# Attention stage of a streaming encoder step: order of copies and sums, masks of the streams by another route, and copies moved in two SSM groups

## The reference, cut to what matters

```python
h = rmsnorm(x, norm_mix[0])
q, k, v, qi, ki, wi = split(h @ w_in)            # attention inputs and indexer inputs
s = einsum('bqhd,bsd->bqhs', qi, keys_i)         # 8 indexer heads
score = einsum('bqhs,bqh->bqs', relu(s), wi) * IDX_SCALE
score = where(k_chunk <= q_chunk, score, -inf)
top_s, top_i = lax.top_k(score, min(256, n_keys // 4))
logits = q . k[top_i] * ATTN_SCALE + bias_tab[rel_bucket(top_i - pos)]
out = softmax(logits) @ v[top_i]                 # 16 heads on 4 key/value heads
x = x + out @ w_o
x = x + square(relu(rmsnorm(x) @ w_up)) @ w_down
h = rmsnorm(x)
xs, B, C, z, dt = conv_silu_split(h @ ssm_w_in)  # 8 groups
y, state = ssd_scan(xs, dt, A, B, C, state0)
x = x + gated_norm(y, z) @ ssm_w_out             # then the second MLP and the last norm
```

## Time and profile before

| | before |
|---|---|
| median of 3 timed runs | 1880.13 us (1877.41 to 1880.49) |
| profiled execution, its own time | 1876.36 us |
| its span | 1874.6 us |
| busy share: PE, DVE, ACT, POOL | 98%, 67%, 43%, 15% |
| mean granted TensorE clock | 0.995 of full |

### The profile page before, as it was taken

The page is one execution under the profiler, slowest core; times in us unless marked ns, Lnnn a source line. Parts: engine busy times, 40 slices in busy tenths (PEclk is TensorE's granted clock), DMA queues, the critical chain, the costliest instruction groups (busy, mean ns, idle before and its releaser), DMA issues.

```text
span 1874.6 us, 35518 instructions
## 1 busy us (share of the span) xinstructions
PE 1834.3 (98%) x13290; PEld 1731.4 (92%) x13290; DVE 1259.0 (67%) x2359; ACT 802.1 (43%) x1436; POOL 290.1 (15%) x336
## 2 busy tenths in 40 slices
PE   8999889999999999999999999999999999999998
PEld 7877556999999999999999999998999999999998
DVE  4488875348668585447788788888444766858653
ACT  4232674334343343335455644556333434434332
POOL 0001541110000000122323434233011000000001
PEclk9999999999999999999999999999999999999999
DMA  6363215232323223222443344434423231322321
GB/s 156 83 109 67 64 36 151 53 90 74 96 63 98 78 68 96 85 57 87 133 120 115 118 131 145 129 116 161 135 78 90 68 102 57 96 74 80 93 66 57
DMA packets 311427, 176.88 MB, mean 94 GB/s; under 512 B 39744, under 2 KB 304896, under 8 KB 310272
## 3 DMA queue, kind: packets, MB, share of 16 engines
q1 hardware_dynamic: 308464, 171.95, 32.5%
q10 hardware_dynamic: 2832, 3.15, 0.5%
HBM read 155.17 MB, written 19.72 MB: 93 GB/s over the span
## 4 chain that ended last, share of the span: by engine, by line
PE 88%; DVE 4%; issue 3%; ACT 3%; DMA 0%; DVEq 0%; POOL 0%; SPq 0%; ACTq 0%
PE psum L208 32%; PE psum L1380 27%; PE psum L1426 14%; PE psum L592 1%; PE psum L2474 1%; PE psum L2567 1%; PE psum L2487 1%; PE psum L556 1%; PE psum L596 1%; PE psum L2501 1%; PE psum L543 1%; PE psum L2405 1%; PE psum L568 1%; PE psum L2591 1%; DVE conv_out L711 0%
## 5 line engine op out<-in xcount | busy, mean ns | idle before, releaser
L208 PE MATMUL psum<-b2H,WH 128*128 128x320 f32 x912 | 218.0, 320 | 0.3 <-DVE b2L L1186 0.3
L208 PE MATMUL psum<-b2H,WL 128*128 128x320 f32 x912 | 209.0, 311 | 0.0
L208 PE MATMUL psum<-b2L,WH 128*128 128x320 f32 x912 | 208.8, 310 | 0.0
L196 ACT ACTIVATE WH<-W 128x1024 fp32r<-128x1024 f32 x90 | 95.1, 1056 | 214.9 <-PE psum L208 207.1
L1380 PE MATMUL psum<-b2H,HT 128*128 128x320 f32 x816 | 186.2, 309 | 0.0
L1380 PE MATMUL psum<-b2L,HT 128*128 128x320 f32 x816 | 186.0, 309 | 0.0
L1426 PE MATMUL psum<-HH,HT 128*128 128x320 f32 x544 | 167.4, 308 | 1.5 <-DVE HL L1515 1.5
L1426 PE MATMUL psum<-HL,HT 128*128 128x320 f32 x544 | 167.8, 308 | 0.0
L208 PEld LDWEIGHTS psum<-b2H,WH 128*128 128x128 f32 x912 | 150.1, 190 | 8.0 <-issue 7.3
L208 PEld LDWEIGHTS psum<-b2H,WL 128*128 128x128 f32 x912 | 153.5, 189 | 0.0
L208 PEld LDWEIGHTS psum<-b2L,WH 128*128 128x128 f32 x912 | 153.4, 189 | 0.0
(11 more groups left out here) (407 smaller groups left out, 4335.4 us busy)
## 6 DMA issues: line engine op xcount, KB each, us to landing
W<-ssm_w_in SPq DMA_DIRECT2D x98, 256.0 KB, 3.1
RW<-mlp_w_up SPq DMA_DIRECT2D x64, 256.0 KB, 3.1
RWx<-mlp_w_up SPq DMA_DIRECT2D x64, 256.0 KB, 3.1
RW<-mlp_w_down SPq DMA_DIRECT2D x64, 256.0 KB, 3.1
RWx<-mlp_w_down SPq DMA_DIRECT2D x64, 256.0 KB, 3.2
bc<-scratch_acs SPq DMA_DIRECT2D x8, 1280.0 KB, 7.7
W<-attn_w_in SPq DMA_DIRECT2D x32, 256.0 KB, 4.0
prev<-state_ssm SPq DMA_DIRECT2D x16, 512.0 KB, 5.6
```

What stands on the lines that cost most here:

```text
L196: act.activation(WH[:, b.slot], W[:, b.slot], ACT.Copy).then_inc(w_hi, 1)
L208: last = pe.matmul(psum[0:m, b.out + h, 0:TH], w[:, b.slot, k, 0:m], r[:, k, h * TH:(h + 1) * TH], start=(n == 0 and i == 0), stop=(n == K ...
```

## The change

**Start.** On ACT x_hi(7) now stands ahead of x_squares(3); on DVE the last chunk_lo stands ahead of the norm's reciprocal. A constant of 512 KB (c_rep) is no longer loaded, nor cast by POOL.

**Q blocks.** The index sums of two samples are made together: Rs has room for two, sum_heads works once per pair of samples and writes rows 0 to 31 and 32 to 63 of one PSUM bank (sel is 32 columns wide, 16 of them zero), copy_scores copies 64 rows once per pair. The top-k's first round reads the scores where they are, without the copy into WK, and its last round leaves out the replacement.

**Prompt attention.** The transposes of two units of a pair with t at most 1 go to one PSUM bank, and one copy takes both. spread_sums moves between the two logits of its step, copy_spread one unit later. scale_heads writes to hF, and heads_hi and heads_lo move into the sample attention, one tile per sample. The samples' top-k has 33 steps in place of 34 and starts without its copy; their mask steps come one unit earlier and write float32 into WKs.

**Sample attention.** The mask product on PE is gone. Instead SP stores the whole mask to memory (264 KB), and for every sample loads the rows with each repeated for its heads (264 KB); POOL adds them to the bias (BMs), two additions of 128x528 per sample, and sample_max takes BMs in place of biasS. The loop over samples is written out.

**SSM.** In the first group Btok is copied ahead of silu_rows(3), in the last one copy_prev(7, 0) ahead of exp_w.

```diff
-            sp.dma_start(rep_stage[:], A["c_rep"].rearrange("p (b r) -> p b r", b=DB)).then_inc(rep_in, 16)
...
+            def load_mask(b):
+                sp.wait_ge(bm, NU + max(2 * b - 2, 0))
+                sp.dma_start(MS[:, b % 2],
+                             skew(S["scores"], DS * b * KEYS_S, [[0, 8], [KEYS_S, DS], [1, KEYS_S]])
+                             ).then_inc((ss_in, bias_in)[b % 2], 16)
+
             sp.wait_ge(mk, 28)
+            sp.dma_start(S["scores"], WKs[:]).then_inc(tb_out, 16)
+            sp.wait_ge(tb_out, 32)
+            load_mask(0)
+            load_mask(1)
             sp.wait_ge(qz, 1)
             for s in range(2):
                 load_v(s, s)
-            with sp.Fori(1, DB // 2) as i:
...
+            for b in range(2, DB):
+                sp.wait_ge(skt, 2 * b - 2)
+                load_k(b, b % 2)
+                load_mask(b)
+                sp.wait_ge(pv, NPV + 2 * b - 2)
+                load_v(b, b % 2)
...
+            def sample_bias(b):
+                pool.wait_ge((ss_in, bias_in)[b % 2], (16, 256)[b % 2] + 16 * (b // 2) + 16)
+                for a in range(2):
+                    if b:
+                        pool.wait_ge(ttr, NU + 2 * b + a - 1)
...
+                    pool.tensor_tensor(BMs[:, a], MS[:, b % 2], biasS[:, a], ALU.add).then_inc(bm, 1)
...
-            def sum_heads(b, bank_=7):
-                pe.wait_ge(iR, b + 2)
-                pe.matmul(psum[0:DS, bank_, 0:512], sel[:], Rs[:, 0:512], start=True, stop=True)
-                pe.matmul(psum[0:DS, 6, 32:32 + DS], sel[:], Rs[:, 512:KEYS_S], start=True, stop=True).then_inc(isl, 1)
+            def sum_heads(i, bank_=7):
+                pe.wait_ge(iR, 2 * i + 3)
+                for s in range(2):
+                    pe.matmul(psum[32 * s:32 * s + 32, bank_, 0:512], sel[:], Rs[:, s, 0:512], start=True, stop=True)
+                for s in range(2):
+                    last = pe.matmul(psum[32 * s:32 * s + 32, 6, 32:32 + DS], sel[:], Rs[:, s, 512:KEYS_S], start=True, stop=True)
+                last.then_inc(isl, 1)
...
                 for q in range(t + 1):
-                    last = pe.transpose(psum[:, 4 + u % 2, q * P:(q + 1) * P], PR[:, u % 4, q * P:(q + 1) * P], ident)
+                    c = (2 * q + gp if in_pair(u) else q) * P
+                    last = pe.transpose(psum[:, turned_bank(u), c:c + P], PR[:, u % 4, q * P:(q + 1) * P], ident)
...
                 if u + 4 < NU:
                     logits(u + 4)
-                    logits(u + 5)
                 if u % 8 == 0 and u:
                     spread_sums(u // 8 - 1)
+                if u + 4 < NU:
+                    logits(u + 5)
...
                 for lo, n in ((0, 512), (512, DS)):
                     out = psum[:, 2 * a + lo // 512, 0:n]
-                    pe.matmul(out, repst[:], maskS[:, lo:lo + n], start=True, stop=False)
-                    last = pe.matmul(out, qst[:, a], kpT[:, a, lo:lo + n], start=False, stop=True)
+                    last = pe.matmul(out, qst[:, a], kpT[:, a, lo:lo + n], start=True, stop=True)
...
             for t in range(NT):
-                if t < 3:
+                if t < 4:
                     x_hi(t + 4)
                 x_squares(t)
...
             norm_act_sqrt(act, 0)
-            x_hi(7)
...
-                if u % 8 == 1 and u > 8:
+                if u % 8 == 2 and u > 8:
                     copy_spread(u // 8 - 1)
-                if u % 8 == 4 and u > 8:
-                    heads_hi(u // 8 - 1)
...
+            for b in range(DB):
+                if b:
+                    sample_heads(b - 1)
                 sample_turned(b)
+                heads_hi(b)
...
+            chunk_lo(dve, 7, 7, 0, b1H, b1L)
             norm_dve_recip(dve, 0)
-            chunk_lo(dve, 7, 7, 0, b1H, b1L)
...
             def sample_max(b, a):
                 dve.wait_ge(qk, NU + 2 * b + a + 1)
+                dve.wait_ge(bm, NU + 2 * b + a + 1)
...
-                dve.tensor_tensor_reduce(PRS[:, a], bank(2 * a, KEYS_S, 2), biasS[:, a], -1.0, -LOWEST,
+                dve.tensor_tensor_reduce(PRS[:, a], bank(2 * a, KEYS_S, 2), BMs[:, a], -1.0, -LOWEST,
...
-        silu_rows(act, g, 3)
+        if not g_is_first(g):
+            silu_rows(act, g, 3)
         act.wait_ge(tB, g + 1)
...
         act.activation(Btok[:], bank(4, T, 2), ACT.Copy).then_inc(bt_, 1)
+        if g_is_first(g):
+            silu_rows(act, g, 3)
...
         exponents(act, g, between)
+        if last:
+            copy_prev(act, SG - 1, 0)
         exp_w(act, g)
```

More of the change, by code:

```diff
@@ L72, in shape_constants @@
     c[:, 640:648] = i[:, None] // DS == np.arange(DB)[None, :]
-    rep = np.zeros((P, DB, P), np.float32)
-    for b in range(DB):
-        for r in range(P):
-            rep[DS * b + r % DS, b, r] = 1.0
-    sel = np.zeros((P, DS), np.float32)
+    sel = np.zeros((P, 32), np.float32)
     sel[i, i % DS] = 1.0
@@ L418, in build, with in_pair, turned_bank, turned_free @@
     NPV = NU // 2
+    def in_pair(u):
+        return UNITS[u][1] <= 1
+    def turned_bank(u):
+        return 4 + (u // 2 % 2 if in_pair(u) else u % 2)
+    def turned_free(u):
+        last = max(p for p in range(u // 2 * 2) if turned_bank(p) == turned_bank(u))
+        return last // 2 * 2 + 2 if in_pair(last) else last + 1
     LAST_PAIR = 3
@@ L2219, in _ @@
                     load_slab(sp, Block(n), slab_o(P * (n - B_O)))
-                if b:
+                if b and b % 2 == 0:
+                    store_scores(b - 2)
                     store_scores(b - 1)
@@ L2440, in mid @@
                     turn_ki(i, s, first and s == 0)
-                    if not (first and s == 0):
-                        sum_heads(2 * i + s - 1)
+                    if not first and s == 0:
+                        sum_heads(i - 1)
                 for s in range(2):
                     multiply(pe, Block(B_Q + s, i), b1H, b1L, between=lambda: mid(s))
-                    index_sample(2 * i + s)
+                    index_sample(i, s)
             q_pair(0, True)
@@ L2522, in _ @@
             turn_kv(0, 4)
-            pe.wait_ge(isc, 2 * DB)
+            pe.wait_ge(isc, DB)
             turn_kv(1, 7)
-            sum_heads(DB - 1, 5)
+            sum_heads(3, 5)
             for u in range(0, NU, 2):
@@ L2712, in copy_ki, with copy_scores @@
                 act.activation(kiP[:, 0:PAST], bank(4), ACT.Copy).then_inc(ik, 1)
[L2714 to L2718 removed]
+            def copy_scores(i, bank_=7):
+                act.wait_ge(isl, i + 2)
+                for s in range(2):
+                    act.wait_ge(iss[s], 16 * i + 16)
+                act.activation(selo[:, 0:512], psum[0:64, bank_, 0:512], ACT.Copy).then_inc(isc, 1)
+                act.activation(selo[:, 512:KEYS_S], psum[0:64, 6, 32:32 + DS], ACT.Copy).then_inc(isc, 1)
             def q_pair(i, first=False):
@@ L2722, in q_pair @@
                     copy_ki(2 * i + s)
-                    if s:
-                        copy_scores(i, 0)
-                    elif not first:
-                        copy_scores(i - 1, 1)
+                    if s == 0 and not first:
+                        copy_scores(i - 1)
                     b = Block(B_Q + 2 + s, i)
@@ L2753, in copy_turned @@
                 _, t, j, gp = UNITS[u]
+                if in_pair(u) and gp == 0:
+                    return
                 act.wait_ge(tp, u + 1)
-                if u == 0:
-                    act.wait_ge(iss[0], 16 * (DB // 2 + 1))
-                if u == 8:
+                if u == 9:
                     act.wait_ge(ss_in, 16)
                 wait(act, pv, u // 2 - 1)
+                if in_pair(u):
+                    act.activation(PT[:, u // 2 % 2, 0:t + 1].rearrange("p t g q -> p (t g q)"),
+                                   bank(turned_bank(u), 2 * P * (t + 1)), ACT.Copy).then_inc(pte, 2)
+                    return
                 act.activation(PT[:, u // 2 % 2, 0:t + 1, gp],
@@ L2764, in copy_spread @@
                 act.wait_ge(rsp, w + 1)
-                wait(act, otl, w)
+                wait(act, oe, w)
                 act.activation(OT[:], bank(7), ACT.Copy).then_inc(rbc, 1)
@@ L2813, in _ @@
             copy_spread(NU // 8 - 1)
-            heads_hi(NU // 8 - 1)
             sample_exp(0, 0)
@@ L2946, in q_block @@
                 split_lo(dve, Block(B_Q + 2 + s, i))
-                weigh_index(2 * i + s)
-            top_round(0)
+                weigh_index(i, s)
+            top_round(0, first=True)
             top_round(1)
@@ L2957, in _ @@
             top_round(14)
-            top_round(15)
+            top_round(15, last=True)
             q_block(3, 1)
@@ L3110, in _ @@
             scale_heads(NU // 8 - 1)
-            heads_lo(NU // 8 - 1)
             sample_max(0, 0)
@@ L3125, in sample_step @@
                 sample_normalize(b)
+                heads_lo(b)
                 if not last:
@@ L3129, in _ @@
             dve.wait_ge(qz, 4)
-            sample_step(0)
```

(3 more changed lines are left out.)

169 lines of the change are left out of this document (75 added, 94 removed).

## The result

| | before | changed |
|---|---|---|
| median of the timed runs | 1879.79 us (1877.41 to 1880.49, 4 runs) | 1860.91 us (1859.92 to 1862.98, 4 runs) |
| ratio | | 0.9911 (0.9896 to 0.9926) |
| span of the profiled execution | 1874.6 us | 1858.1 us |

The change saves 18.9 us where 31.6 were forecast. The time is inside the range by 0.1 us, but by the ratio (0.9911 of 1880.13 is 1863.4) it is outside. It is a gain, and six tenths of the forecast one by the medians; by the ratio it is 16.7 us, and the two traces differ by 16.5. One execution of a later run, start_undone, took 8286.73 us and is left out of its ratio.

The account below looks back on a forecast made before the run. PE, busy 98% of the span, was taken as the bound. Terms 5.2 + 5.3 + 8.0 + 5.5 + 3.7 + 3.8 = 31.5 us off 1876.4, plus 3.8 for the median, gave 1848.5 us; range 1842 to 1861.

Parts of the forecast that it names:

- Start: First stage: x_hi(7) earlier removes PE's 1.8 us wait for b1L and 3.4 us of lower clock, 5.2 us.
- Q blocks: Index sums made in pairs save 4.0 us, the vanished wait for Rs 1.3: 5.3 us (1.3 to 5.3).
- the rival of tiles in a row: Q blocks: a pair's products in two column tiles run one after another, 4.0 us stay, 1852.5 us; chance 0.07.
- the forecast's own bound: Q blocks: if paired sums run in a row, 7 single become 3 double ones and 1.0 us of saving remains.
- Prompt attention: PE's 16 waits for exponentials at seven tile boundaries go: 8.0 us (5 to 9.5).
- with spreading half a step earlier on PE: Prompt attention: this and the copy one unit later give ACT another exponential meanwhile, part of the 8.0 us.
- Sample attention: Mask products gone from PE save 4.3 us, the stage's start 1.2: 5.5 us (2 to 6).
- the 1.2 at the start: Sample attention's start: 1.2 us saved because heads_lo no longer stands there.
- the 0 to -1 that was named: Sample attention's start: possible loss of 0 to 1 us by the chain of mask store, load and POOL's addition.
- SSM: Waits for Btok (first group) and prevT (last group) shrink, with the clock behind them: 3.7 and 3.8 us.
- the waits go over to DVE or to POOL's chain: Prompt attention gives only 3 of 8.0 us, sample attention 2 of 5.5: 1857 us; chance 0.22.
- The clock still drops: Lower clock stays at the start and both SSM places, up to 6.8 us lost: 1850 to 1855 us; chance 0.15.

Follow-up runs that it names:

- start_undone: Changed kernel with the first stage's old order (x_hi(7) behind the square root, last chunk_lo behind the reciprocal): 1864.65 us, ratio 0.9935.
- before_rows: Kernel before the change, with the SSM's skip weights read as 128 packets of 64 bytes, not 2,048 of 4; also called the control: 1876.7 us, ratio 1.0001.
- copy_back: best_guess with copy_spread one unit earlier on ACT, where it was before the change: 1857.28 us, ratio 0.9896.
- d_in_rows: Changed kernel with the SSM's skip weights read as 128 packets of 64 bytes, not 2,048 of 4 (skip values wrong): 1854.26 us, ratio 0.9877.
- fill: Changed kernel with 18 transposes into an unused bank in PE's waits at the end of the sample attention: 1853.25 us, ratio 0.9875.
- d_split: Changed kernel with the second half of the skip weights' 4-byte load issued behind the last W_o slab: 1851.62 us, ratio 0.9864.
- best_guess: Changed kernel with spread_sums behind both logits, skip weights' load in two halves apart, second mask's load behind the values: 1849.34 us, ratio 0.9858.
- spread_first: Changed kernel with spread_sums ahead of both logits of its step: 1860.02 us, ratio 0.9909.
- spread_behind: Changed kernel with spread_sums back behind both logits of its step: 1859.65 us, ratio 0.9903.

## Why the prediction was right in its parts and wrong in its sum

- **Start (5.2, measured 5.9).** Right: the wait and the lower clock behind it are gone, and come back with the order. The size holds within a microsecond only, since the same wait was followed by 3.4 us at the lower clock in before_rows and by 6.8 in the kernel before.
- **Q blocks (5.3, measured 6.1).** Right. A pair of sums in two column tiles takes 1.05 us, x4 (the row above), where a single one took 1.03, x2; the rival of tiles in a row is out. Its price was wrong by the forecast's own bound, which leaves 1.0 of the 4.0: 3.0 would have stayed, not 4.0.
- **Prompt attention (8.0, measured 4.2).** Half of the mechanism was right, and by copy_back its size too: the copy one unit later is worth 8.5. The step that failed is "with spreading half a step earlier on PE": I took it as a help at no price. PE's two logits of a pair use rows 0 to 63 and 64 to 127 and run side by side; set between them, spread_sums makes each run alone. Undone, the stretch is 3.6 us shorter, and 7.8 shorter than before the change, where 8.0 were forecast. In the Q blocks I had asked whether two narrow products run side by side, and here I did not ask what the move would part, though the x4 rows of the trace show it.
- **Sample attention (5.5, measured 3.7).** A size: a round is 6.49 us where it was 7.03, so 0.54 less, as forecast (twice 0.27), but in six rounds only; they gave 3.2, against 4.3 forecast for the mask products of eight; and of the 1.2 at the start 0.5 is left, since 0.85 went into DVE's wait for POOL, within the 0 to -1 that was named. The load took 4.6 us rather than the 2.8 of the earlier trace rows, the store 2.1 rather than 2.8. All eight heads_lo took 0.69 us, and none fell beside an addition of POOL, so whether the two exclude each other was not put to the test here.
- **W_o (0, measured -8.8).** The step that failed, and the one that cost the most, is the sum's silence: a stage that isn't changed was taken as fixed, at nothing, without a reason. 5.5 us of wait and 1.7 of clock behind it come from the fetch of PE's instructions, held back for some 17 us by 4-byte packets (d_in_rows, fill, d_split and the control show it). The earlier trace rows show what stands behind such packets, 19.7 us for a load of 16 KB, and the prediction used that row for the masks only. The other 1.6, the clock at the start of W_o, is lower in some executions: 0.67 in the changed kernel's profile, 1.00 in best_guess, with the same waits of PE ahead (0.54, 0.36, 0.75 and 0.99 us), and before_rows has it as well, without any of the change. The two are not quite a sum: spread_first and start_undone have the full clock there, but a wait of 5.9, and take 36.3 and 36.0 us where the changed kernel takes 37.0. So the fetch alone costs 7.7 to 8.1, and the clock at the start adds 0.7 to 1.0 more.
- **SSM (7.5, measured 7.1).** Right: prevT's wait became 0.47, for the states, 0.4 having been forecast.
- **The rest (0, measured -1.7).** The MLPs run 1.2 and 0.5 us longer over 500 us each. The offset of 3.8 between the profiled execution and the median was 1.0 for the changed kernel. And the forecast's 1844.9 + 3.8 is 1848.7, not 1848.5. No experiment here tells the first two from chance.

With the two failed steps at what was measured, 31.5 - 3.6 - 7.2 = 20.7 and less the 1.8 in the sample attention 18.9, which is the gain by the medians; that it fits to the digit is luck, as the clock's 1.6 and the surplus of the first stages cancel, and by the ratio the gain is 16.7. Of the rivals, "the waits go over to DVE or to POOL's chain" had 0.22 and a time of 1857; its amount in the prompt attention was about right and its cause wrong: neither DVE nor POOL is what held PE. "The clock still drops" did not come true in its three places, but in two others. No rival named what cost the most.

## What to carry to other kernels

When an instruction is moved on PE, look at what stands on both sides of the gap: two products on different rows or columns of the array cost the time of one here, and with other products between the two of a pair on different rows they cost the time of two. Before transfers in packets of 4 bytes are laid beside straight-line code, ask which engine's next instructions fall due in that time; keep a run of such packets short (here two of 10 us did no harm where one of 20 cost 7 us) or read the data in rows. A wait labelled "issue" in the middle of unbroken work, with weights and inputs there, is worth a look at the instruction queues of the DMA view.

## What the runs showed of the hardware

- 2,048 packets of 4 bytes ran at about 106 per us from 309 to 329 us and kept the 16 DMA engines busy for 4.7% of their time. Still, what came behind, two loads of 16 KB and the packet of queue 8, landed only when they were nearly done (20.7 us for the first, against 2.9 without them). One packet of instructions of another queue, 14, did get through at 315.0 us.
- PE ran on for about 14 us (an estimate, above) after the fetch that was held back had fallen due.
- The granted clock behind like waits of PE is not the same from one execution to the next. After waits of 0.39, 0.88 and 0.96 us at the prompt attention's head, d_in_rows and spread_behind had 0.58 from 175 to 180 us, the changed kernel, fill and best_guess 1.00; that is some 2.6 us, as much as some of the terms that one would like to tell apart. At the start of W_o, behind the waits named above, seven of the twelve profiles without filling have the lower clock and five don't.
